# A hybrid decoder step on one core: nine more constant turns, two sums moved behind other tiles, a split last sum, output stored by halves

## The reference, cut to what matters

```python
h = x + concat(conformer_conv(A), rg_lru(B)) @ w_out      # A, B: parts of rmsnorm(x) @ w_in + b_in
h = h + hier_moe(rmsnorm(h))                              # 32 experts, top 2 of one group for each token
gate = sigmoid(rmsnorm(h, ple_norm_g) @ w_pg + b_pg)      # w_pg: 2048 x 2048
h = h + gate * (p @ w_ple)
y = rmsnorm(h, final_g)                                   # y_prompt (256 x 2048), y_sample (8 x 2048)
```

## Time and profile before

| what | us |
|---|---|
| three runs | 1496.03, 1497.32, 1501.69 (median 1497.32) |
| the profiled execution's own time | 1497.86 |
| its span, first to last instruction | 1496.0 |
| outside the span | 1.86 |
| TensorE busy in the span | 1427.9 |

### The profile page before, as it was taken

The page is one execution under the profiler, slowest core; times in us unless marked ns, Lnnn a source line. Parts: engine busy times, 40 slices in busy tenths (PEclk is TensorE's granted clock), DMA queues, the critical chain, the costliest instruction groups (busy, mean ns, idle before and its releaser), DMA issues. The chain is left out here.

```text
span 1496.0 us, 17840 instructions
## 1 busy us (share of the span) xinstructions
PE 1427.9 (95%) x7469; PEld 827.5 (55%) x7469; DVE 637.2 (43%) x1248; ACT 227.0 (15%) x383; POOL 127.2 (9%) x113
## 2 busy tenths in 40 slices
PE   9999999999999999999999999999999999997996
PEld 7888887899863343343334333433343334334996
DVE  5698854754552232223223322322232223226775
ACT  3000046733310000000000000000000000004342
POOL 1000002242000000000000000000000000000241
PEclk8999999999999999999999999999999999999998
DMA  9945340365479999999999999999999999996461
GB/s 270 309 155 202 122 113 1 97 172 175 191 302 412 424 428 427 429 427 427 427 428 428 427 428 429 427 426 427 428 428 428 427 428 428 427 424 189 133 173 63
DMA packets 122202, 482.63 MB, mean 323 GB/s; under 512 B 5241, under 2 KB 87713, under 8 KB 96610
## 3 DMA queue, kind: packets, MB, share of 16 engines
q1 hardware_dynamic: 120778, 475.45, 80.0%
q0 software_dynamic: 912, 2.89, 0.7%
q10 hardware_dynamic: 432, 3.15, 0.5%
HBM read 479.06 MB, written 3.42 MB: 323 GB/s over the span
## 5 line engine op out<-in xcount | busy, mean ns | idle before, releaser
L1012 PE MATMUL ps<-ring,xwin 128*64 128x512 f32 x1984 | 452.5, 597 | 25.5 <-DMA ring<-in_w_up_dram 25.5
L1738 DVE TENSOR_TENSOR hT<-hT,ps 128x528 f32<-128x528 f32 x256 | 171.6, 702 | 354.2 <-PE ps L976 350.8
L1012 PEld LDWEIGHTS ps<-ring,xwin 128*64 128x64 f32 x1984 | 140.6, 136 | 286.9 <-issue 286.9
L1034 PE MATMUL ps<-ring,hid 128*64 128x512 f32 x1024 | 236.6, 616 | 0.0
L700 PE MATMUL ps<-xT,ring 128*128 128x264 f32 x1024 | 232.4, 389 | 0.0
L700 PEld LDWEIGHTS ps<-xT,ring 128*128 128x128 f32 x1024 | 196.0, 192 | 33.8
L976 PE MATMUL ps<-sel,ysb 64*128 64x264 f32 x1024 | 184.8, 415 | 1.5 <-DVE ysb L1730 0.8
L976 PEld LDWEIGHTS ps<-sel,ysb 64*128 64x128 f32 x1024 | 103.5, 186 | 111.1 <-issue 100.6
L1034 PEld LDWEIGHTS ps<-ring,hid 128*64 128x64 f32 x1024 | 72.7, 141 | 146.9 <-issue 136.0
L647 POOL COPY xwin<-xTs 128x1024 f32 x31 | 32.4, 1046 | 837.9 <-PE ps L1012 819.4
L1287 ACT ACTIVATE sgl<-ps 64x512 f32<-64x512 f32 x32 | 18.8, 588 | 526.2 <-PE ps L1012 526.2
(11 more groups left out here) (341 smaller groups left out, 1272.5 us busy)
## 6 DMA issues: line engine op xcount, KB each, us to landing
ring<-in_w_gate_dram SPq DMA_DIRECT2D x64, 2048.0 KB, 16.0
ring<-in_w_up_dram SPq DMA_DIRECT2D x64, 2048.0 KB, 20.5
ring<-in_w_down_dram SPq DMA_DIRECT2D x64, 2048.0 KB, 18.2
ring<-in_w_in_dram SPq DMA_DIRECT2D x32, 512.0 KB, 8.7
ring<-in_w_in_dram SPq DMA_DIRECT2D x16, 1024.0 KB, 8.0
ring<-in_w_out_dram SPq DMA_DIRECT2D x16, 1024.0 KB, 5.8
ring<-in_w_pg_dram SPq DMA_DIRECT2D x16, 1024.0 KB, 5.9
ring<-in_w_ple_dram SPq DMA_DIRECT2D x2, 1024.0 KB, 4.8
```

The costliest lines, as they stand in the source:

```text
L1012: mm = pe.matmul(ps[part * WIN:(part + 1) * WIN, 0, :], window(k), weights(2 * j + part)[:, kk * F:(kk + 1) * F], start=(k == 0), stop=(k ...
L1034: mm = pe.matmul(ps[half * WIN:(half + 1) * WIN, 2 + b, :], hid[:, t, :], weights(8 + t)[:, q * 512:(q + 1) * 512], start=(t == 0), stop=( ...
L1738: dve.tensor_tensor(pair, pair, ps[:, b:b + 2, 0:TOK], ALU.add).then_inc(sems["added"], 1)
```

## The change

1. Ahead of `rb_ready`, PE turns the constant nine more times (`WARM // 4`), into a bank that nothing reads before tile 1 of the projection.
2. `mean` is asked behind tile 24 instead of 23.
3. The sum of squares is asked behind w_pg tile 1 instead of tile 0.
4. Tile 12 is turned back behind tile 14 and tile 13 behind tile 15; DVE takes tile 13 before the last `gate_out`. POOL adds only the first 14 squares. PE sums `acc4`, then the square of tile 14, turns back tile 15, and sums the square of tile 15.
5. Prompt rows are scaled by halves of 1024 columns, DVE's before the sample rows, and each half is stored as it is ready, all five transfers from SP.

```diff
-BACK = {..., 12: (7, 8), 13: (9, 10), 14: (11,), 15: (12,)}
+BACK = {..., 12: (7, 8), 13: (9, 10), 14: (11, 12), 15: (13,)}
...
-        for c in (2, 0):
-            sp.wait_ge(y_ready, 1 if c == 2 else 2)
-            dst = o["y_prompt"][0, c * P:(c + 1) * P, :] if c < 2 else o["y_sample"][:, 0, :]
-            sp.dma_start(dst, ring[0:ROWS[c], Y_SLOTS[c], :]).then_inc(out_done, 16)
-        sp.wait_ge(out_done, 48)
+        for h in range(2):
+            sp.wait_ge(y_ready, h + 1)
+            store(0, h)
+            sp.wait_ge(y_act, h + 1)
+            store(1, h)
+        sp.wait_ge(y_ready, 3)
+        sp.dma_start(o["y_sample"][:, 0, :], ring[0:NB, Y_SLOTS[2], :]).then_inc(out_done, 16)
+        sp.wait_ge(out_done, 80)
...
-        for m in range(KD):
+        for m in range(KD - 2):
             add_square(m, sqt, acc4, sq4_ready, sq4_summed)
...
+        for _ in range(WARM // 4):
+            pe.transpose(ps[:, 1, 0:P], ident[:, :], ident[:, :])
         pe.wait_ge(rb_ready, 1)
...
-            if n == 23:
+            if n == 24:
                 mean()
...
-            if m == 0:
+            if m == 1:
                 pe.wait_ge(sq3_summed, 2 * UNITS)
...
-        for m in range(KD - 3, KD):
-            turn_back(m)
-        pe.wait_ge(sq4_summed, KD)
-        for c in range(3):
-            r = ROWS[c]
-            mm = pe.matmul(ps[0:r, 5, c:c + 1], acc4[:, c * P:c * P + r], ones[:, 0:1], start=(c == 0), ...)
-        mm.then_inc(sum4_full, 1)
+        turn_back(KD - 2)
+        pe.wait_ge(sq4_summed, KD - 2)
+        sum_square(acc4[:, :], True)
+        pe.wait_ge(sq4_ready, KD - 1)
+        sum_square(sqt[:, 0, :], False)
+        turn_back(KD - 1)
+        pe.wait_ge(sq4_ready, KD)
+        sum_square(sqt[:, 1, :], False).then_inc(sum4_full, 1)
...
-        act.activation(ring[:, Y_SLOTS[1], :], ring[:, Y_SLOTS[1], :], ACT.Copy, scale=rstd[:, 1:2]).then_inc(y_act, 1)
-        act.wait_ge(y_act, 1)
-        act.dma_start(o["y_prompt"][0, P:2 * P, :], ring[:, Y_SLOTS[1], :]).then_inc(out_done, 16)
+        for h in range(2):
+            cols = slice(h * DC, (h + 1) * DC)
+            act.activation(ring[:, Y_SLOTS[1], cols], ring[:, Y_SLOTS[1], cols], ACT.Copy, scale=rstd[:, 1:2])\
+                .then_inc(y_act, 1)
...
-            gate_out(m)
+            if m < KD - 1:
+                gate_out(m)
             for b in BACK.get(m, ()):
                 take_back(b)
-        for m in range(KD - 3, KD):
+        gate_out(KD - 1)
+        for m in range(KD - 2, KD):
             take_back(m)
...
-        for c in (2, 0):
+        for c, cols in ((0, slice(0, DC)), (0, slice(DC, D)), (2, slice(0, D))):
```

More of the change, by code:

```diff
@@ L41 @@
 GATE_BANK = (0, 1, 2, 6)
-BACK = {**{m: (m - 5,) for m in range(5, 12)}, 12: (7, 8), 13: (9, 10), 14: (11,), 15: (12,)}
+BACK = {**{m: (m - 5,) for m in range(5, 12)}, 12: (7, 8), 13: (9, 10), 14: (11, 12), 15: (13,)}
 MIX_FIRST = list(range(TC, KD - 1))
@@ L545, in _, with store @@
             load_tile(KD + t)
-        for c in (2, 0):
-            sp.wait_ge(y_ready, 1 if c == 2 else 2)
-            dst = o["y_prompt"][0, c * P:(c + 1) * P, :] if c < 2 else o["y_sample"][:, 0, :]
-            sp.dma_start(dst, ring[0:ROWS[c], Y_SLOTS[c], :]).then_inc(out_done, 16)
-        sp.wait_ge(out_done, 48)
+        def store(c, h):
+            cols = slice(h * DC, (h + 1) * DC)
+            sp.dma_start(o["y_prompt"][0, c * P:(c + 1) * P, cols], ring[:, Y_SLOTS[c], cols]).then_inc(out_done, 16)
+        for h in range(2):
[6 more added lines that the diff above has]
+        sp.wait_ge(out_done, 80)
     @block.gpsimd
@@ L1118, in _, with sum_square @@
                 turn_back(b)
-        for m in range(KD - 3, KD):
-            turn_back(m)
-        pe.wait_ge(sq4_summed, KD)
-        for c in range(3):
-            r = ROWS[c]
-            mm = pe.matmul(ps[0:r, 5, c:c + 1], acc4[:, c * P:c * P + r], ones[:, 0:1], start=(c == 0), stop=True,
-                           skip_group_check=True)
-        mm.then_inc(sum4_full, 1)
+        def sum_square(part, first):
+            for c in range(3):
+                r = ROWS[c]
+                mm = pe.matmul(ps[0:r, 5, c:c + 1], part[:, c * P:c * P + r], ones[:, 0:1], start=(first and c == 0),
+                               stop=True, skip_group_check=True)
+            return mm
+        turn_back(KD - 2)
[6 more added lines that the diff above has]
+        sum_square(sqt[:, 1, :], False).then_inc(sum4_full, 1)
     @block.scalar
@@ L1840, in _ @@
         inverse_root(3, 4)
-        for c in (2, 0):
+        for c, cols in ((0, slice(0, DC)), (0, slice(DC, D)), (2, slice(0, D))):
             r = ROWS[c]
-            dve.tensor_scalar(ring[0:r, Y_SLOTS[c], :], ring[0:r, Y_SLOTS[c], :], rstd[0:r, c:c + 1], None, ALU.mult)\
+            dve.tensor_scalar(ring[0:r, Y_SLOTS[c], cols], ring[0:r, Y_SLOTS[c], cols], rstd[0:r, c:c + 1], None, ALU.mult)\
                 .then_inc(y_ready, 1)
```

## The result

| what | before | after |
|---|---|---|
| runs, measured side by side | 16 | 16 |
| median of the runs (us) | 1498.9 | 1491.1 |
| lowest and highest (us) | 1494.18, 1503.54 | 1488.06, 1496.24 |
| the profiled execution (us) | 1497.86 | 1494.06 |
| its span (us) | 1496.0 | 1492.1 |

The ratio of after to before is 0.9948, interval 0.9936 to 0.996. The change makes the kernel faster by 7.8 us (of the medians), a little more than half of the 14.1 forecast, and the time lies 1.1 above the upper end of the range.

A forecast was written before the change was run, and what follows sets the result against it. With TensorE busy 1427.9 of 1496.0 us, gains lay in PE's idle time, its clock, the start and the end. 3.6 + 0 + 7.5 + 3.0 = 14.1 us from 1497.86 gave 1483.8, range 1480.5 to 1490.0.

The forecast's parts named there:

- the landing of the states: At the start, the states' load was taken to land at 29.8 us, so 3.6 us won; ends 0.2 and 5.2.
- The other half of that step: At the start, nine constant turns hold PE's full clock without delaying `rb`; PE would reach the state turns 5.2 us earlier.
- Rival 1: At the start, the clock falls anyway and `rb` comes 0.7 us late: 1488.1 us, chance 0.28.
- The sum behind tile 1: In the w_pg stage, asking the sum of squares one tile later removes PE's wait and its low-clock tail: 7.5 us won.
- Rival 2: In the w_pg stage, the sum still comes late for DVE: 1.6 us won instead of 7.5, 1489.7 us, chance 0.06.
- The mean: Mean product moved behind projection tile 24, to about 212 us, ahead of DVE's read at 220.79: 0 us.
- The end: After the last `gate_in`: 2.0 us won up to the scaling, 0.4 lost by a turn-back, 1.4 won in stores: 3.0.
- the rate of 303: Output stores from SP's queue alone at 303 GB/s would take 7.1 us and lose 0.5, the stores' lower end.
- the clock in the stages that the change doesn't touch: Stages outside the edited places: the forecast sum has no term for clock changes there.
- Rival 3: Among the experts, the earlier start puts a clock fall into each of 32: slower, 1503.0 us, chance 0.04.

The follow-up runs named there:

- e1: The kernel before with only the nine turns of the constant added: 1500.24 us, ratio 1.0015 to before.
- e5: The kernel before with only the mean asked behind tile 24 instead of 23: 1499.63 us, ratio 0.9996 to before.
- e8: The whole change run again without any edit, beside the kernel before: 1490.91 us, ratio 0.9949.
- e6: The whole change with the states turned one projection tile later, behind tiles 1 and 2: 1486.05 us, ratio 0.9904 to before.
- e9: The same program as e6, run once more beside the kernel before: 1483.54 us, ratio 0.9909.
- e10: The same program as e7, run once more beside the kernel before: 1487.57 us, ratio 0.9925.
- e7: The whole change with the states turned one tile later, but without the nine turns: 1489.12 us, ratio 0.9926 to before.
- e2: The kernel before with only the sum of squares asked behind w_pg tile 1: 1490.98 us, ratio 0.9954 to before.
- e4: The whole change without the nine turns: 1490.12 us, ratio 0.9932 to the kernel before.

## Why the prediction was wrong, and where it was right

**The first step that failed is the landing of the states: "I take 29.8, so 3.6 us are won".** `lstage`, issued at 18.76, released PE at 32.93, and in the other profiles with a wait for it at 32.77 (e1), 31.98 (e5) and 31.64 (e8). This is the lower end that the prediction named ("0.2 if they land just ahead of 33.4"), not the value it took: 0.5 won instead of 3.6.

For the kernel before, 29.8 was nearly right. No row above shows a landing that nobody waited for, but the trace also keeps the counts of the semaphore `late_rows`. Where PE waited, the last count comes 0.04 us ahead of PE's start; in before it comes at 30.81. The packets of the states run there from 22.9 to 30.0, so the dip in the rate was read rightly, too. What failed is the premise that the landing stays where it was. In the five profiles with the nine turns (after, e1, e6, e8, e9) the last count comes at 31.60 to 32.89, on average 32.4; in the seven without them at 29.80 to 31.93, on average 30.7. From before to after it moved by 2.1 us, so of the 3.1 that are missing about 1 is the size and 2 the move. The fourth chunk of `w_in`, ahead of the states in the queue, moved alike: its last count comes at 26.96 to 27.62 with the turns and at 24.81 to 25.93 without. In e1 PE stood 1.26 us for it inside tile 0, where the prediction had put nothing.

What delays these loads was not tried and stays open. One thing in the traces goes with it: a 16 KB packet of instructions, 1.1 to 1.3 us long, is moved at 19.8 to 21.3 in the five profiles with the turns and at 25.4 to 31.8 in the seven without. That the packet holds the loads up is a guess.

By itself this step would have made the forecast 1483.8 + 3.1 = 1486.9, which lies inside the stated range; the second step that failed stands further below.

**The other half of that step was right.** In e1, e6 and e9 the nine turns hold the clock, and a gain behind `rb` arrives once the states are moved: 3.4 between e10 and e9. That this is close to the 3.6 is luck: the 3.6 was cut short by the landing, and without it the prediction had 5.2. In e9 0.5 of that went into the wait for the fourth chunk, and in e10 there was less to win, with the lower clock from 17.2 to 27.4 where before had it from 15.0 to 28.6. Rival 1, "the clock falls anyway", is not what happened in general. In after and in e8 the clock did fall, but at 11.7 and 12.1, ahead of the nine turns and behind waits of 2.04 and 1.76 us for x, a delay that the profile of before (0.28) doesn't show (e6 waited 1.72 and kept the clock). Even there the clock was up again for the turns of x and for tile 0; the landing set the end in both.

The Trainium skill (TensorE: Matmul & The Clock Gate, Part 4: PE-mode transpose) says that the full clock doesn't engage for transposes. e1 contradicts it for turns of the constant and of x alike: 1.00 from 15.60 to 28.30 us, of which the first five us are turns and the products on `rb` only. By that rule the first state turn of e6 would have come no earlier than that of e7; they came at 36.0 and 39.7.

**The sum behind tile 1**: 7.5 forecast, 30.2 - 22.1 = 8.1 in the trace of after and in that of e2. The mechanism was right, with its tail (PEclk 1.00 for 0.52), and DVE had 1.8 us to spare where 1.4 were forecast. The 0.6 too little is the tile: I took 7.36, the length of a merged row, for each; two tiles in a row took 14.48 and the third let the next work start after 6.92. Rival 2 is out.

**The mean**: 0 forecast, 0.9996 alone. PE ran it at 210.8; DVE came to it at 220.4.

**The end**: 3.0 forecast. The trace of after gives 1.95 (forecast 2.0) up to the scaling, 1.3 (1.4) in the stores, less 0.4 for the turn-back, 2.8. The stores flowed at 402 GB/s from one queue, so the rate of 303 that set the lower end didn't come.

**The second step that failed is a term that the sum put at nothing: the clock in the stages that the change doesn't touch.** Stage by stage, the profile of after against that of before has -0.5 at the start, -8.1 at w_pg, +0.4 and -3.2 at the end; against them +1.6 behind the fall at 254, and for the group of falls +1.6 from the router to the gather (21.8 against 20.2), +3.1 from there through the first expert (54.3 against 51.2) and +1.7 from the last expert's last product on `xwin` to w_pg (21.2 against 19.5). All the rest takes 0.5 less. Together that is -3.9, the difference of the spans. Rival 3 had the right kind of loss at the wrong place: it asked for a fall in each expert; there were five in after outside the group, as many as before had beside its first.

The turns (e4 has the group without them, e1 not), the mean (e5 doesn't have it) and the moved states (e6 has it, e9 not) don't decide the group. All four profiles that show it (after, e4, e6, e8) hold parts 3 to 5, but these act only from 1376 us on, and e7, e9 and e10 hold them without it. What does decide it is open. All 28 runs of the change took 1488.06 or more, and e8's profiled one, with the group, 1490.95; without it I estimate 1490.95 - 6.4 = 1484.6, which no run reached. Only two profiles of the change show the group, and how many of its executions have it is not shown. One of e8's runs, 1488.95, had a mean granted clock of 0.992: some 24 us at the lower level, where the group (17) and the end behind 1482.9 (9) make 26 in after. So that run can't have had the whole group, and it is no faster than its neighbours; the group alone need not be what keeps the runs above 1488. With the landing as it is (3.1) and the group (6.4) the forecast of 1483.8 would have been 1493.3; the profiled execution took 1494.06, the median of the runs is 1491.1.

## What to carry to other kernels

A wait that no row shows has no time: if an engine came after a transfer, its rows say only that the transfer had landed by then, and a gain that ends at that transfer is worth between nothing and its size. Nor need the landing stay where it was: here it came 1.7 us later on average in the profiles with the nine turns. Before making a stretch faster, list what the engine asks for next and when each of these lands; here asking for the states one tile later (e6, e9) took the mean of the runs from 1491.7 to 1485.6. And a product that waits for another engine is best put behind work that needs no wait: in the trace one line won 8 us, 5 of waiting and 3 of the lower clock behind it.

## What the runs showed of the hardware

Two executions of one program differed by 5.9 us because PE's clock fell to 1.2 GHz in other places: behind 380 us, in the first and in the last expert (0.76, 0.63 and 0.89 in e6's stretches; 1.00, 0.88 and 1.00 in e9's). A profile of one execution doesn't tell how often that happens. The falls inside the other experts cost nothing in the end: e6 had six there and e9 two, and PE in e6 was 4.6 us behind e9 when it left the first expert (453.66 against 449.08) and 4.3 behind near the end of the experts (1332.31 against 1328.04), where it waited for `w_up` in both.

A load of 96 KB, issued at 18.76 behind 1 MB chunks, released its reader 14.2 us later in after; the same load of before, issued at 18.82, had landed 12.0 us later.

The add into hT took 0.92 next to POOL's add and 0.43 without it, as the prediction took from a row of another stage.
